# One large kernel of four transformer layers: attention's probabilities are divided before they are turned, and the odd mixer's levels are merged by predicated copies

## What is computed

```python
def _softmax_attend(q, k, v):
    s = jnp.einsum('bhgqd,bhkd->bhgqk', q, k, preferred_element_type=jnp.float32) * (ATT_HEAD_DIM ** -0.5)
    p = jax.nn.softmax(s, axis=-1).astype(v.dtype)
    return jnp.einsum('bhgqk,bhkd->bhgqd', p, v)

# one step of _chunk_gla, the recurrence of _odd_mixer
decay = jnp.exp(jnp.where(tri, G[:, :, :, None, :] - G[:, :, None, :, :], -jnp.inf))
scores = jnp.einsum('bhik,bhjk,bhijk->bhij', qc, kc, decay)
o = jnp.einsum('bhij,bhjv->bhiv', scores, vc) + jnp.einsum('bhik,bhkv->bhiv', qc * jnp.exp(G), s)

# second block, layer 1: a softmax over a window with one sink per head
m = jnp.maximum(jnp.max(logits, axis=-1, keepdims=True), sink)
e = jnp.exp(logits - m)
probs = e / (jnp.sum(e, axis=-1, keepdims=True) + jnp.exp(sink - m))
```

## Time and profile before

| | us |
|---|---|
| median of 3 runs | 3252.39 |
| lowest, highest | 3248.42, 3252.47 |
| profiled execution | 3252.44 |
| its span | 3250.4 |
| PE busy | 3061.9 (94%) |
| VectorE busy | 766.0 (24%) |
| ScalarE busy | 411.6 (13%) |
| GpSimd busy | 289.2 (9%) |

### The profile page before, as it was taken

One profiled execution on the slowest core, in us unless ns is written; L12 is line 12 of the kernel. 1 busy time (PEld: TensorE's weight loads), 2 busy tenths in 40 slices (PEclk: granted clock), 3 DMA queues, 4 the chain that ended last, 5 costly groups with the idle time before them and its releaser, 6 DMA issues.

```text
span 3250.4 us, 41429 instructions
## 1 busy us (share of the span) xinstructions
PE 3061.9 (94%) x18032; PEld 1733.6 (53%) x18032; DVE 766.0 (24%) x1653; ACT 411.6 (13%) x1012; POOL 289.2 (9%) x354
## 2 busy tenths in 40 slices
PE   6989889999989999899998999998999999999998
PEld 2456644444447777567656777454444444444443
DVE  1136822000035676510033000243000000000002
ACT  1014221000022222210022000130000000000001
POOL 1022300000012233200000000000000000000030
PEclk9999989999999999999989999998999999999998
DMA  8670012122122112152443333326999999999992
GB/s 340 253 289 7 2 63 79 40 97 78 39 61 66 52 46 78 59 188 97 155 168 117 136 136 138 128 70 244 362 403 375 376 406 377 376 403 380 374 403 86
DMA packets 211812, 613.33 MB, mean 189 GB/s; under 512 B 6252, under 2 KB 53580, under 8 KB 205104
## 3 DMA queue, kind: packets, MB, share of 16 engines
q1 hardware_dynamic: 204912, 592.20, 48.0%
q0 software_dynamic: 6256, 17.87, 1.6%
q10 hardware_dynamic: 464, 0.60, 0.1%
HBM read 603.43 MB, written 7.21 MB: 188 GB/s over the span
## 4 chain that ended last, share of the span: by engine, by line
PE 86%; DVE 7%; issue 2%; DMA 2%; ACT 2%; POOL 0%; POOLq 0%; ACTq 0%; SPq 0%; DVEq 0%
PE ps_ffn_gate L612 10%; PE ps_ffn_up L612 10%; PE ps_ffn_down L648 10%; PE ps_moe_down L3061 6%; PE ps_moe_gate L3016 6%; PE ps_moe_up L3016 6%; PE ps_odd L1924 4%; PE ps_lin L1403 4%; PE ps_project L530 3%; PE ps_moe_down L3067 3%; PE ps_moe_up L3021 3%; PE ps_moe_gate L3021 3%; PE ps_lin L298 3%; PE ps_ple_gate L2597 2%; DVE rec_qd L2183 2%
## 5 line engine op out<-in xcount | busy, mean ns | idle before, releaser
L612 PE MATMUL ps_ffn_gate<-hT,ring_buf 128*128 128x256 f32 (+1 forms) x1152 | 343.7, 452 | 4.3 <-issue 2.4
L612 PE MATMUL ps_ffn_up<-hT,ring_buf 128*128 128x256 f32 (+1 forms) x1152 | 336.7, 445 | 1.3
L648 PE MATMUL ps_ffn_down<-ring_buf,ffn_hiddenT 128*128 128x512 f32 x752 | 325.9, 593 | 3.1 <-issue 3.1
L612 PEld LDWEIGHTS ps_ffn_gate<-hT,ring_buf 128*128 128x128 f32 x1152 | 222.1, 194 | 120.5 <-issue 99.1
L612 PEld LDWEIGHTS ps_ffn_up<-hT,ring_buf 128*128 128x128 f32 x1152 | 217.9, 190 | 110.3 <-issue 90.0
L1924 PE MATMUL ps_odd<-ring_buf,hT 128*128 128x256 f32 (+2 forms) x1024 | 236.0, 385 | 8.0 <-ACT hg_kT L2059 6.4
L648 PEld LDWEIGHTS ps_ffn_down<-ring_buf,ffn_hiddenT 128*128 128x128 f32 x752 | 141.7, 190 | 182.1 <-issue 182.1
L697 DVE TENSOR_TENSOR ffn_hiddenT<-ffn_silu_buf,ps_ffn_up 128x256 f32<-128x256 f32 (+1 forms) x72 | 36.2, 503 | 727.4 <-PE ps_ffn_up L612 727.4
L1924 PEld LDWEIGHTS ps_odd<-ring_buf,hT 128*128 128x128 f32 x1024 | 173.7, 192 | 55.1 <-ACT hg_kT L2059 7.9
L3199 DVE TENSOR_TENSOR moe_hidden_buf<-moe_silu_buf,ps_moe_up 128x768 f32<-128x768 f32 (+1 forms) x32 | 27.3, 854 | 679.3 <-PE ps_moe_up L3021 679.3
L3061 PE MATMUL ps_moe_down<-ring_buf,moe_hiddenT 128*64 128x512 f32 x640 | 142.4, 595 | 5.4 <-ACT moe_hiddenT L3136 4.0
(11 more groups left out here) (519 smaller groups left out, 3448.0 us busy)
## 6 DMA issues: line engine op xcount, KB each, us to landing
ring_buf<-in_w_exp_down_dram SPq DMA_DIRECT2D x17, 4096.0 KB, 16.6
ring_buf<-in_w_exp_up_dram SPq DMA_DIRECT2D x16, 4096.0 KB, 16.9
ring_buf<-in_w_exp_gate_dram SPq DMA_DIRECT2D x15, 4096.0 KB, 18.1
mod_pieces<-in_mod_w_dram SPq DMA_DIRECT2D x40, 1024.0 KB, 6.5
moe_third<-in_w_exp_gate_dram SPq DMA_DIRECT2D x9, 4096.0 KB, 17.9
moe_third<-in_w_exp_up_dram SPq DMA_DIRECT2D x8, 4096.0 KB, 18.0
moe_third<-in_w_exp_down_dram SPq DMA_DIRECT2D x7, 4096.0 KB, 17.1
ring_buf<-in_odd_w_in_dram SPq DMA_DIRECT2D x40, 512.0 KB, 5.3
```

Of the source, the lines that this page charges most:

```text
L612: mm = nc.tensor.matmul(ps[:, 0:wide], view[:, k, i * P:(i + 1) * P], hT[:, k, first_col:first_col + wide], start=k == 0, stop=k == KD - 1)
L648: mm = nc.tensor.matmul(ps_y[i % 2][:, h, :], hidT[:, b, i * P:(i + 1) * P], view[:, b, h * 512:(h + 1) * 512], start=first, stop=end)
```

## The change

*Attention.* The two scaled identities are gone. VectorE takes the reciprocal as before and multiplies the probabilities themselves by it, in place, one instruction for each head over all its keys (`shares`). PE turns them by `transpose` with the plain identity.

*Odd mixer.* Masks, halves and sums of a unit become one function `merge` on VectorE. The first two levels are multiplied by their masks into two places; the next three pairs of levels are put over them by `copy_predicated`, where the mask isn't zero. The eight levels end in two 128x128 places, and PE multiplies both with the values and adds in PSUM, one matmul more per unit. GpSimd's `halves` is gone.

```diff
@@ attend, tensor engine: turned(u)
-                    pe.wait_ge(S["att_probs"].handle, S["att_probs"].at(u + 1))
-                    pe.wait_ge(S["att_diag"].handle, S["att_diag"].at(u + 1))
+                    pe.wait_ge(S["att_shares"].handle, S["att_shares"].at(u + 1))
                     pe.wait_ge(S["att_T_ready_a"].handle, S["att_T_ready_a"].at(u))
                     pe.wait_ge(S["att_T_ready_v"].handle, S["att_T_ready_v"].at(u))
                     for h in range(2):
                         for k in range(len(keys_of(u))):
-                            mm = nc.tensor.matmul(ps_t[:, h, k, :], probs[:, u % 2, h, k * P:(k + 1) * P], diag[:, u % 2, h, :],
-                                                  start=True, stop=True)
+                            mm = nc.tensor.transpose(ps_t[:, h, k, :], probs[:, u % 2, h, k * P:(k + 1) * P], ident)
@@ attend, vector engine
-                def diagonal(u):
+                def shares(u):
+                    nk = len(keys_of(u)) * P
                     total, inverse = stat[:, u % 4, 1, :], stat[:, u % 4, 2, :]
                     dve.wait_ge(S["att_probs"].handle, S["att_probs"].at(u + 1))
                     link_v(nc.vector.reciprocal(inverse, total))
                     for h in range(2):
-                        last = nc.vector.tensor_scalar(diag[:, u % 2, h, :], ident, stat[:, u % 4, 2, h:h + 1], None, ALU.mult)
-                    last.then_inc(S["att_diag"].handle, 1)
+                        mine = probs[:, u % 2, h, 0:nk]
+                        last = nc.vector.tensor_scalar(mine, mine, stat[:, u % 4, 2, h:h + 1], None, ALU.mult)
+                    last.then_inc(S["att_shares"].handle, 1)
@@ odd_mixer, gpsimd
-                def halves(U):
-                    pool.wait_ge(S["rec_masked"].handle, S["rec_masked"].at(U + 1))
-                    nc.gpsimd.tensor_tensor(masked[:, 0:4, :], masked[:, 0:4, :], masked[:, 4:8, :], ALU.add)\
-                        .then_inc(S["rec_halved"].handle, 1)
@@ odd_mixer, tensor engine: output(U)
-                    pe.wait_ge(S["rec_summed"].handle, S["rec_summed"].at(U + 1))
+                    pe.wait_ge(S["rec_masked"].handle, S["rec_masked"].at(U + 1))
...
-                    mm = nc.tensor.matmul(ps_out, summed[:, U % 2, :], v_of(U), start=False, stop=True)
+                    for s in range(PLACES):
+                        mm = nc.tensor.matmul(ps_out, merged[:, U % 2, s, :], v_of(U), start=False, stop=s == PLACES - 1)
@@ odd_mixer, vector engine
-                def mask(U):
+                def merge(U):
+
+                    made_by, mine = scores_of(U), merged[:, U % 2, :, :]
                     dve.wait_ge(S["rec_scores"].handle, S["rec_scores"].at(U + 1))
-                    dve.wait_ge(S["rec_summed"].handle, S["rec_summed"].at(U))
-                    nc.vector.tensor_tensor(masked[:, :, :], scores_of(U), mask_table[:, UNITS[U % 4][0], :, :],
-                                            ALU.mult).then_inc(S["rec_masked"].handle, 1)
-
-                def add_levels(U):
-                    dve.wait_ge(S["rec_halved"].handle, S["rec_halved"].at(U + 1))
                     if U >= 2:
                         dve.wait_ge(S["rec_out"].handle, S["rec_out"].at(U - 1))
-                    nc.vector.tensor_reduce(summed[:, U % 2, :], masked[:, 0:4, :].rearrange("p l n -> p n l"), AX.X,
-                                            ALU.add).then_inc(S["rec_summed"].handle, 1)
+                    for r in range(ROUNDS):
+                        levels = slice(r * PLACES, (r + 1) * PLACES)
+                        which = mask_table[:, UNITS[U % 4][0], levels, :]
+                        if r == 0:
+                            last = nc.vector.tensor_tensor(mine, made_by[:, levels, :], which, ALU.mult)
+                        else:
+                            last = nc.vector.copy_predicated(mine, which.bitcast(I32), made_by[:, levels, :])
+                        if r < ROUNDS - 1:
+                            link_v(last)
+                    last.then_inc(S["rec_masked"].handle, 1)
```

More of the change, by code:

```diff
@@ L1003, in program @@
         ("att_staged", "tensor"), ("att_q_ready", "scalar"), ("att_k_ready", "vector"), ("att_scores", "tensor"),
-        ("att_max", "vector"), ("att_probs", "scalar"), ("att_diag", "vector"), ("att_turned", "tensor"),
+        ("att_max", "vector"), ("att_probs", "scalar"), ("att_shares", "vector"), ("att_turned", "tensor"),
         ("att_T_ready_a", "scalar"), ("att_T_ready_v", "vector"), ("att_out", "tensor"), ("att_taken", "scalar"))}
@@ L1031, in attend @@
             probs = sb(cx, "att_probs_buf", [P, 2, 2, nkt * P + own_column])
-            diag = sb(cx, "att_diag_buf", [P, 2, 2, P])
             masked = sb(cx, "att_masked", [P, 2, 2, nkt * P + own_column]) if mask is not None else None
@@ L1204, in _ @@
                     if 1 <= i <= n:
-                        diagonal(i - 1)
+                        shares(i - 1)
                     if i >= 2:
                         take_turned(i - 2)
-            for k in ("att_scores", "att_max", "att_probs", "att_diag", "att_turned", "att_T_ready_a", "att_T_ready_v",
+            for k in ("att_scores", "att_max", "att_probs", "att_shares", "att_turned", "att_T_ready_a", "att_T_ready_v",
                       "att_out", "att_taken"):
@@ L1757, in odd_mixer @@
             kd = tail(1, 4096, 2 * (NL - 2) * 2 * P).rearrange("p (d l n) -> p d l n", d=2, l=NL - 2)
-            masked = tail(2, 4096, NL * P).rearrange("p (l n) -> p l n", l=NL)
+            PLACES, ROUNDS = 2, NL // 2
+            merged = tail(2, 4096, 2 * PLACES * P).rearrange("p (b s n) -> p b s n", b=2, s=PLACES)
             vs = tail(2, 5120, 1024).rearrange("p (b t n) -> p b t n", b=2, t=4)
             part = tail(2, 6144, 512).rearrange("p (b n) -> p b n", b=2)
-            summed = tail(2, 6656, 256).rearrange("p (b n) -> p b n", b=2)
             small = sb(cx, "rec_block_products", [P, 240])
@@ L1868, in _ @@
                         roots(h - 1)
-                    for i in range(4):
-                        halves(4 * h + i)
                 roots(HH - 1)
@@ L2253, in _ @@
                         forget(h + 1, 0)
-                    mask(u)
+                    merge(u)
                     if more:
                         forget(h + 1, 1)
-                    add_levels(u)
                     if h == HH - 1:
                         readout(h - 1)
-                    mask(u + 1)
+                    merge(u + 1)
                     take(u)
-                    add_levels(u + 1)
-                    mask(u + 2)
+                    merge(u + 2)
                     if more:
@@ L2266, in _ @@
                     take(u + 1)
-                    add_levels(u + 2)
-                    mask(u + 3)
+                    merge(u + 3)
                     if 1 <= h < HH - 1:
                         readout(h - 1)
-                    add_levels(u + 3)
                     if more:
@@ L2281, in _ @@
                 readout(HH - 1)
-            for k in ("rec_scores", "rec_masked", "rec_halved", "rec_summed", "rec_out", "rec_state"):
+            for k in ("rec_scores", "rec_masked", "rec_out", "rec_state"):
                 S[k].passed(HH * 4)
```

## The result

The changed kernel takes 3230.82 us in the median of 4 runs (3226.16 to 3231.5), against 3252.43 for the kernel before (4 runs). The ratio is 0.9927, with a 95% interval of 0.9915 to 0.9938: 23.7 us faster, by 20 to 28. The two medians alone are 21.6 us apart; the interval holds both. The forecast was 3237.7, a gain of 14.7 us. The sign was right and the gain was under-sized: on the 3252.4 of the forecast the ratio gives 3228.7 us, just under the lower end of the range, 3229, while the median itself lies just inside. The profiled execution took 3231.5 us.

The account below looks back on a forecast made before the run. PE, with 86% of the chain, was taken to bound the kernel. From 3252.4 us, attention's -13.0 and the odd mixer's -1.7 gave 3237.7 us, with a range of 3229 to 3260.

Parts of the forecast that it names:

- the halved records: Attention on PE: transposes need half the matmuls' records, saving 0.90 us per four-key unit, 21.4 us if PE alone set the pace.
- shares at 483 ns for 512 columns: Attention on VectorE: in-place division priced like a 512-column TENSOR_SCALAR between SBUF tiles, 483 ns, with 692 as the other end.
- the predicated copy of 256 columns: Odd mixer on VectorE: each of three copies per unit priced at 0.46 us, 0.49 with its link.
- no wait of PE for the merged levels: Odd mixer: PE's wait at the head of each output, 9.5 us in 14 cases, was to go.
- the wait for the decayed queries: Odd mixer: PE's other wait, 8.4 us in 7 cases, was to stay as it is.
- the added matmul: Odd mixer on PE: one more fp32 matmul of 128 columns per output, 32 x 0.225 = +7.2 us.
- first call: First attention call: 5.1 us kept on four-key units and 2.8 on two-key units, together -7.9 us.
- odd mixer: Odd mixer net: waits at -8.9 us against the extra matmul's +7.2, giving -1.7 us, from -2.3 to +7.2.
- the odd mixer's waits: Odd mixer: PE's 9.5 us of waits go, less 0.1 us a head for switching groups, giving -8.9 us.
- VectorE's hold on attention: First call: VectorE becomes the bound at about 3.0 us per four-key unit, so 0.64 of 0.90 us is kept.
- "About half" for the second and third call: Second and third attention calls: about half of 5.3 us counted, -2.8 in the second, -2.3 in the third.
- The clock: Rival for the attention calls: transposes and gaps drop PE to 1.2 GHz; one call lost gives some 3260 us; chance 0.16.

Follow-up runs that it names:

- mixed places: The changed kernel with two places only for the second unit of each odd-mixer head and one for the others; ratio 0.9914 to the kernel before, median 3227.09 us.
- one place multiplied: The kernel before with the odd-mixer change alone, but the output multiplies only the first of two places, leaving out the second's levels; ratio 0.9949.
- matmuls with in-place shares: The kernel before with attention's probabilities divided in place on VectorE, but turned by fp32 matmuls against the identity instead of transposes; ratio 0.9997.
- doubled transposes: The kernel before with the attention change alone, each transpose issued twice into the same place; ratio 0.9993.
- one place: The changed kernel with the odd mixer's eight levels merged into one place by seven 128-column predicated copies, one matmul from it per output; ratio 0.9919 to before.
- short shares: The kernel before with the attention change alone, but VectorE divides only each unit's first key tile, 128 columns; ratio 1.0341, first call 52.9 us.
- VectorE loaded: Two kernels with attention alone changed: divisions doubled, with transposes, ratio 1.0054; divisions preceded by two multiplications by one, with matmuls against the identity, ratio 1.0147.

## Where the prediction was right and where not

Right: PE as the bound; the halved records (the period fell by 0.96 us, 3.64 to 2.68, where VectorE wasn't in the way, against 0.90); shares at 483 ns for 512 columns, as the row for the same form had it; the predicated copy of 256 columns at 444 ns against 460; no wait of PE for the merged levels; the wait for the decayed queries unchanged; the added matmul at 0.22 us, unhidden.

At equal clock the parts gave this (the second call from attention alone; the third from the mixed places' trace, 36.9 us with no time at the lower level, against 40.6; the odd mixer reckoned from its heads, where the odd change alone measured -6.3 for the stage):

| part | forecast | at equal clock |
|---|---|---|
| first call | -7.9 | -9.0 |
| second call | -2.8 | -4.6 |
| third call | -2.3 | -3.7 |
| odd mixer | -1.7 | -6.1 (7 heads at -1.00, the last at +0.88) |
| sum | -14.7 | -23.4 |

**The step that failed most** is the odd mixer's waits, -8.9 us. I took their idle figures (9.5 us in 14 cases) and even left 0.1 us a head as a cost of switching (7 heads make that -8.8; the -8.9 is a slip of 0.1). Start to start they were worth 7 x 1.88 = 13.2 us. The matmul's +7.2 was right (32 x 0.22 = 7.0), so a term of -8.9 in place of -13.2 is nearly the whole miss of 4.4 us on this part, and half of the miss of 8.7 us on the sum. The run with one place multiplied shows both sizes apart.

**VectorE's hold on attention** was set too tight. I charged all eight four-key units with maxima over 1024 columns (1.14 us start to start) and so kept 0.64 of 0.90 us each. Half of them have 512-column maxima behind them, and two shares take 0.79 us, not 0.9. The mean of the changed kernel's first four periods is 2.76 us (2.82, 2.90, 2.65, 2.68), and with VectorE freed the call gained only 0.7 to 1.1 us more. This term is 1.1 us of the miss.

**"About half" for the second and third call** had no row behind it. PE's waits for VectorE did grow, in the third call from 2.7 us in 6 cases to this:

```profile
PE ps_att_t L1082 <- DVE att_probsT L1182: 5.0, 10, 0.9
```

That takes 2.3 of the 5.3 us that the records give, and leaves 3.0; 3.7 were measured. Counting the new waits would have been the better step than halving. The 0.28 us a wait of the odd mixer's outputs doesn't carry over: four more waits at that price would leave 1.9. These two calls are 3.2 us of the miss.

**The clock** did not turn the result. In brackets the stage table has 10.2 us less 3.4 in the second call, for us, and 4.1 and 3.3 more in and behind the third, against us, with 6.2 more in and behind the even mixer's recurrence, which the odd change alone and the matmuls with in-place shares have as well (13.6 and 13.8 us there). Counting all stretches at 1.2 GHz, before and after have 160 us each. Between kernels with the same attention, a further us at the lower level made a call some 0.35 us longer (the second 43.3 us against 40.9 for 6.8 us more, the third 40.6 against 36.9 for 10.2 us more). But the rival was nearer than its 0.16 said for the third call. Where PE had as many records as before it spent no time at the lower level in four kernels (before, one place multiplied, matmuls with shares, doubled transposes) and 6.8 us in a fifth (the odd change alone); with the halved records 4.1 us after, 10.2 with attention alone, 13.6 with one place and with short shares, none with mixed places. At 10.2 us it took 40.6 us, what it took before: the gain there and the clock's loss are equal.

The Trainium skill, "TensorE: Matmul & The Clock Gate", section "Part 4: PE-mode transpose", by which the full clock doesn't engage in transpose mode, spoke for a loss. The run with doubled transposes is against it in this mix, where transposes stand between matmuls: PEclk 1.00 for 39.10 us. No run here holds a long stretch of transposes alone.

## What to carry to other kernels

Price a wait that is to go from the start of the record ahead of it to the start of the record behind it, not by its idle figure: here 14 waits of 9.5 us in all were worth 13.2. Count the slack of each unit by itself, with everything that stands in the helping engine's queue behind the lengthened step: one size for all four units lost most of what a mixed one kept. And where the bounding engine gets faster beside one that is nearly full, its new waits can cost twice, in time and in its clock.

## What was not expected of the hardware

- With VectorE loaded, PE was idle for 8 to 12 of 49 to 59 us in the second and third call, never for more than 2.1 us at a time, and spent 20 to 34 us of each at 1.2 GHz; in the first call it was idle for 10 to 12 of 48 to 59 us behind its start and stayed at 2.4 GHz.
- The second call had 3.4, 6.8, 10.2 or 13.6 us at the lower level in different kernels without the added work on VectorE, and with the attention of before took 40.9, 43.3 and 44.8 us by it. A change elsewhere in the kernel can so move a stage that it doesn't touch by 2 to 4 us.
- A predicated copy from PSUM took 444 ns for 256 columns and 737 for 512; seven of 128, linked, took 2.31 us.
- A TENSOR_SCALAR in place over 512 fp32 columns took no longer than one between two tiles, 483 ns, and the next instruction started 0.40 us after its start.
